# A macaron decoder layer on one core: paired matmuls in a new order, row sums at later pieces, and extra matmuls on a constant tile at the start

## The reference, cut to what matters

```python
def rmsnorm(x, gain):
    inv = lax.rsqrt(jnp.mean(xf * xf, axis=-1, keepdims=True) + EPS)
    return (xf * inv * gain)
def swiglu(h, w_gate, w_up, w_down):
    return (jax.nn.silu(h @ w_gate) * (h @ w_up)) @ w_down
...
x = x + 0.5 * swiglu(rmsnorm(x, norm_ffn1), w1_gate, w1_up, w1_down)
h = rmsnorm(x, norm_mix)
q, k, v, u = split(h @ w_in)             # 8 heads of 128, and 4 pooling groups of 256
attn = attention(rope(q), rope(k), v)    # causal over the 256 tokens
pooled = multiscale_pool(u, pool_w, pool_scale)
x = x + concatenate([attn, pooled]) @ w_out
x = x + 0.5 * swiglu(rmsnorm(x, norm_ffn2), w2_gate, w2_up, w2_down)
return rmsnorm(x, norm_final)
```

## Time and profile before

| | |
|---|---|
| median of 3 runs | 1843.48 us (1834.06, 1843.48, 1844.43) |
| profiled execution, its own time | 1844.73 us |
| span of that execution, first to last instruction | 1842.9 us |
| PE busy | 1807.6 us, 98% of the span |
| DVE, ACT, POOL busy | 1064.7, 853.8, 57.0 us |
| mean granted TensorE clock | 0.993 |

### The profile page before, as it was taken

How to read it: one execution, slowest core, us unless ns; L and a number is a source line. 1 busy time by engine, 2 the same in 40 slices (tenths; PEclk the granted TensorE clock), 3 DMA queues, 4 the chain that set the end, 5 groups by cost and what they waited for, 6 DMA issues and landing times.

```text
span 1842.9 us, 26110 instructions
## 1 busy us (share of the span) xinstructions
PE 1807.6 (98%) x10134; PEld 1566.5 (85%) x10134; DVE 1064.7 (58%) x1073; ACT 853.8 (46%) x993; POOL 57.0 (3%) x56
## 2 busy tenths in 40 slices
PE   6999999999999999999999999999999999999997
PEld 5888888888888888888787888888888888888886
DVE  5655555555555555577665656555555555545453
ACT  5444444444444444444544554444444444444443
POOL 2000000000000000000030010000000000000000
PEclk9999999999999999999999999999999999999999
DMA  7455555555555656756534555555555555565552
GB/s 253 161 185 188 190 188 182 182 183 184 185 160 183 190 178 188 241 185 193 170 124 128 187 187 179 187 191 186 182 182 184 187 189 172 170 183 183 187 187 91
DMA packets 214377, 333.41 MB, mean 181 GB/s; under 512 B 6104, under 2 KB 97472, under 8 KB 214336
## 3 DMA queue, kind: packets, MB, share of 16 engines
q1 hardware_dynamic: 212624, 331.37, 56.2%
q10 hardware_dynamic: 1712, 1.48, 0.3%
HBM read 330.73 MB, written 2.10 MB: 181 GB/s over the span
## 4 chain that ended last, share of the span: by engine, by line
PE 96%; DVE 1%; ACT 1%; issue 1%; DMA 1%; POOL 0%; SPq 0%
PE banks L330 61%; PE banks L332 31%; PE banks L424 1%; PE banks L422 1%; PE banks L423 1%; DMA raw<-in_w_gate 1%; PE banks L471 0%; PE banks L435 0%; ACT w_hi L564 0%; DVE w_lo L800 0%; POOL square_sum L1127 0%; PE banks L545 0%; PE banks L352 0%; PE banks L457 0%; ACT squares L590 0%
## 5 line engine op out<-in xcount | busy, mean ns | idle before, releaser
L800 DVE TENSOR_TENSOR w_lo<-raw,w_hi 128x1024 fp32r<-128x1024 f32 (+1 forms) x704 | 781.8, 1115 | 734.2 <-ACT w_hi L564 733.7
L330 PE MATMUL banks<-act,w_hi 128*128 128x512 f32 x3200 | 1135.3, 400 | 9.7 <-DVE u L854 2.9
L564 ACT ACTIVATE w_hi<-raw 128x1024 fp32r<-128x1024 f32 (+1 forms) x704 | 677.8, 963 | 947.3 <-PE banks L332 912.9
L332 PE MATMUL banks<-act,w_lo 128*128 128x256 f32 x3200 | 901.1, 282 | 0.0
L330 PEld LDWEIGHTS banks<-act,w_hi 128*128 128x128 f32 x3200 | 604.1, 189 | 159.2 <-DVE u L854 3.1
L332 PEld LDWEIGHTS banks<-act,w_lo 128*128 128x128 f32 x3200 | 608.1, 190 | 0.0
L330 PE MATMUL banks<-h,w_hi 128*128 128x512 f32 x1664 | 589.9, 400 | 3.5 <-DVE u L854 3.5
L332 PE MATMUL banks<-h,w_lo 128*128 128x256 f32 x1664 | 468.4, 282 | 0.0
L330 PEld LDWEIGHTS banks<-h,w_hi 128*128 128x128 f32 x1664 | 313.5, 188 | 81.9 <-DVE u L854 3.9
L332 PEld LDWEIGHTS banks<-h,w_lo 128*128 128x128 f32 x1664 | 315.6, 190 | 0.0
L854 DVE TENSOR_TENSOR h<-banks,h 128x1024 f32 (+1 forms) x44 | 53.7, 1220 | 0.7 <-ACT h L570 0.4
(11 more groups left out here) (111 smaller groups left out, 411.1 us busy)
## 6 DMA issues: line engine op xcount, KB each, us to landing
raw<-in_w_up SPq DMA_DIRECT2D x88, 1024.0 KB, 5.2
raw<-in_w_gate SPq DMA_DIRECT2D x87, 1024.0 KB, 5.2
raw<-in_w_down SPq DMA_DIRECT2D x64, 768.0 KB, 4.5
raw<-in_w_down SPq DMA_DIRECT2D x64, 640.0 KB, 4.2
raw<-in_w_in SPq DMA_DIRECT2D x32, 1024.0 KB, 5.4
raw<-in_w_out SPq DMA_DIRECT2D x16, 1024.0 KB, 5.0
rows<-in_x SPq DMA_DIRECT2D x4, 512.0 KB, 7.6
out<-rows SPq DMA_DIRECT2D x4, 512.0 KB, 3.1
```

The source lines that it names most:

```text
L330: pe.matmul(banks[:, bank + b, :], w_hi[:, s, w], operand[:, k, :], start=first, stop=last, skip_group_check=True)
L332: mm = pe.matmul(banks[:, bank + b, 0:S], w_lo[:, s, w], operand[:, k, 0:S], start=False, stop=last, skip_group_check=True)
L564: act_e.activation(w_hi[:, s, 0:n], raw[:, (p // 2) % RAW_SLOTS, off:off + n], ACT.Copy).then_inc(hi_ready, 1)
L800: dve.tensor_tensor(w_lo[:, s, 0:n], raw[:, (p // 2) % RAW_SLOTS, off:off + n], w_hi[:, s, 0:n].bitcast(F32), ALU.subtract)\
```

## The change

1. Inside a piece, PE issues for each output block first the long matmuls of all its channel blocks and then the short ones, in place of long, short, long, short.
2. In the first gate turn of both feed-forwards PE goes on with up pieces 8 to 11, then takes the sum (now in bank 0, once quad 0 has been read out), then pieces 12 to 15, and waits for the mean behind piece 15. DVE takes the mean behind piece 14 and the inverse behind piece 15; ACT takes the root behind piece 15 and the SiLU behind that. The middle's sum moves from behind Q0's last piece to behind K0's fourth, and the first rotation steps on DVE move with it.
3. DVE sets two tiles of `h` to 1.0 first of all. PE runs 7 matmuls on them (128 weight columns, 512 moving) ahead of the first transpose, and 4 more with 127 weight columns between the first 16 transposes and the first piece. Their products, in bank 3, are overwritten.

The core of the diff:

```diff
@@ multiply (PE), called for every piece
                 for b in range(width // P):
+                    cols = [slice(j * width + b * P, j * width + (b + 1) * P)
+                            for j in range(len(tiles))]
                     for j, k in enumerate(tiles):
-                        w = slice(j * width + b * P, j * width + (b + 1) * P)
-                        first, last = k == k_first, k == last_tile
-                        pe.matmul(banks[:, bank + b, :], w_hi[:, s, w], operand[:, k, :],
-                                  start=first, stop=last, skip_group_check=True)
-                        mm = pe.matmul(banks[:, bank + b, 0:S], w_lo[:, s, w],
-                                       operand[:, k, 0:S], start=False, stop=last,
+                        pe.matmul(banks[:, bank + b, :], w_hi[:, s, cols[j]], operand[:, k, :],
+                                  start=k == k_first, stop=k == last_tile, skip_group_check=True)
+                    for j, k in enumerate(tiles):
+                        mm = pe.matmul(banks[:, bank + b, 0:S], w_lo[:, s, cols[j]],
+                                       operand[:, k, 0:S], start=False, stop=k == last_tile,
                                        skip_group_check=True)
@@ gate_up (PE)
-                if first:
-
-                    if f["turn"]:
-                        pe.wait_ge(quad_read, m)
-                    sum_squares(0 if f["turn"] == 0 else 2, False)
...
-                        pe.wait_ge(gains_ready, 2)
-                    pe.wait_ge(meansq_ready, 1 if f["turn"] == 0 else 3)
+                if f["turn"] or not first:
+                    pe.wait_ge(quad_read, m)
                 else:
-                    pe.wait_ge(quad_read, m)
+                    pe.wait_ge(x_copied, 8)
                 for p in range(8, 16):
                     multiply_sb(turn, p, 1)
+                    if first and p == 11:
+                        pe.wait_ge(quad_read, m + 1)
+                        sum_squares(0 if f["turn"] == 0 else 2, False)
...
+                if first:
+
+                    pe.wait_ge(meansq_ready, 1 if f["turn"] == 0 else 3)
+                    if f["turn"] == 0:
+                        pe.wait_ge(gains_ready, 2)
@@ middle (PE)
-                        if p == K0:
+                        if p == Q1:
 
                             pe.wait_ge(meansq_ready, 2)
...
-                        if p == K0 - 1:
-                            pe.wait_ge(quad_read, MID_SB)
+                        if p == K0 + 3:
+                            pe.wait_ge(quad_read, MID_SB + 1)
                             sum_squares(1, True)
@@ the start (PE)
+            def warm(count, cols):
+
+                for _ in range(count):
+                    pe.matmul(banks[0:cols, 3, :], h[:, FT - 1, 0:cols], h[:, FT - 2, :],
+                              start=True, stop=True)
+
+            pe.wait_ge(warm_ready, 1)
+            warm(7, P)
             pe.wait_ge(first_const_landed, 16 * 2)
...
             turn_x(1)
+            warm(4, P - 1)
@@ gate_up (ACT)
-                    if first and p == 11:
-                        square_roots(0 if fresh else 2)
-                    if p == 14:
+                    if p == 14 and not first:
                         silu(SB * i)
+                if first:
+
+                    square_roots(0 if fresh else 2)
+                    act_e.wait_ge(gate_scaled, fi + 1)
+                    silu(SB * i)
@@ gate_up (DVE)
-                    if first and p == 10:
+                    if first and p == 14:
                         mean_square(norm)
...
-                    if p == 12:
+                    if p == (15 if first else 12):
                         if first:
                             inverse_root(norm)
@@ middle (DVE; ACT's square_roots(1) moves from p == 11 to p == 15)
-                    if p == 10:
+                    if p == 14:
                         mean_square(1)
...
-                    if 11 <= p < K1 + 16 and 3 <= p % 8 <= 7:
+                    if 19 <= p < K1 + 16 and 3 <= p % 8 <= 7:
                         rotate((p - 11) // 8, p % 8 - 3)
+                    if p in FIRST_ROTATE:
+                        rotate(0, FIRST_ROTATE.index(p))
@@ the start (DVE), and the tables
+            dve.memset(h[:, FT - 2:FT, :].bitcast(F32), 1.0).then_inc(warm_ready, 1)
+SUM_BANK = (0, 0, 0, 4)
+FIRST_ROTATE = (11, 15, 16, 17, 18)
```

More of the change, by code:

```diff
@@ L165, in layer_kernel @@
         ones_ready = sem("ones_ready")
+        warm_ready = sem("warm_ready")
         gains_turned = sem("gains_turned")
@@ L348, in sum_squares @@
                 pe.wait_ge(ones_ready, 1)
-                b = 4
+                b = SUM_BANK[norm]
                 if norm < 3:
@@ L383, in gate_up @@
                     multiply_sb(turn, p, 0, act_from=f["act"] if first else None)
-                if first:
-                    if f["turn"]:
-                        pe.wait_ge(quad_read, m)
-                    sum_squares(0 if f["turn"] == 0 else 2, False)
[L389 to L392, removed]
-                        pe.wait_ge(gains_ready, 2)
-                    pe.wait_ge(meansq_ready, 1 if f["turn"] == 0 else 3)
+                if f["turn"] or not first:
+                    pe.wait_ge(quad_read, m)
                 else:
-                    pe.wait_ge(quad_read, m)
+                    pe.wait_ge(x_copied, 8)
                 for p in range(8, 16):
                     multiply_sb(turn, p, 1)
+                    if first and p == 11:
+                        pe.wait_ge(quad_read, m + 1)
+                        sum_squares(0 if f["turn"] == 0 else 2, False)
+                        if f["turn"] == 0:
+                            pe.wait_ge(const_landed, 16 * 4)
+                            pe.transpose(banks[:, 1, 0:3 * KT + 8], gain_rows[:, :],
+                                         ident[0:3 * KT + 8, 0:3 * KT + 8]).then_inc(gains_turned, 1)
+                if first:
+                    pe.wait_ge(meansq_ready, 1 if f["turn"] == 0 else 3)
+                    if f["turn"] == 0:
+                        pe.wait_ge(gains_ready, 2)
             def down_two(f, i):
@@ L706, in middle @@
                         pair_update(ffns[0], KT - 2, DOWN_PAIRS - 1, MID_TURN * TURN, 1)
-                    if p == 11:
+                    if p == 15:
                         square_roots(1)
@@ L816, in mean_square @@
                 if norm in COL_NORMS:
-                    ins = dve.tensor_scalar(r_col[:, :], banks[:, 4, S:S + 2], 1.0 / D, EPS,
+                    ins = dve.tensor_scalar(r_col[:, :], banks[:, SUM_BANK[norm], S:S + 2], 1.0 / D, EPS,
                                             ALU.mult, ALU.add)
                 if norm in ROW_NORMS:
-                    ins = dve.tensor_scalar(r_row[:, :], banks[:, 4, 0:S], 1.0 / D, EPS,
+                    ins = dve.tensor_scalar(r_row[:, :], banks[:, SUM_BANK[norm], 0:S], 1.0 / D, EPS,
                                             ALU.mult, ALU.add)
@@ L870, in gate_up @@
                         feed(0, 2 * p, 2, 2 * p)
[L871 to L874, removed]
                     if first and f["turn"] and p in (3, 6):
@@ L880, in gate_up @@
                         split_h(SB * i - SB, fi)
-                    if first and p == 10:
+                    if first and p == 14:
                         mean_square(norm)
+                        if fresh:
+                            dve.wait_ge(gains_turned, 2)
+                            dve.tensor_copy(gains[:, KT:4 * KT + 8],
+                                            banks[:, 1, 0:3 * KT + 8]).then_inc(gains_ready, 1)
                     if p == 11:
                         add_half(0, h32[:, bass.ds(SB * i, SB), 0:S], m + 1, m + 1)
-                    if p == 12:
+                    if p == (15 if first else 12):
                         if first:
```

## The result

The changed kernel took 1814.65 us (median of 4 runs, 1812.41 to 1815.50; the profiled execution 1815.50, span 1813.7). The kernel before took 1838.77 us in the 4 runs beside it (1828.75 to 1844.43). The ratio of comparable runs is 0.992 with a 95% interval of 0.9892 to 0.9949: a gain of some 0.8%. Against the medians it is 1.3%, and against the one execution of before that was profiled 1.6%. That these three differ is the main finding of this study: the kernel before has three times, not one. (By that ratio before stands at some 1829 us, near the lowest of its four runs, 1828.75; a run list is therefore given wherever it matters.)

A forecast was written before the change was run, and what follows sets the result against it. PE, busy 98% of the span, bounds the kernel through how it issues and where it stands still. 1844.73 - 8.9 (first sum) + 0.5 (lateness) - 1.2 (other sums) - 29.9 (runs of two) = 1805 us; range 1798 to 1836.

The forecast's parts named there:

- The 0.70: Chance given to the changed kernel being faster, meaning a time below 1825 us.
- Two paces at one clock, drawn at a restart and kept: PE's long-short pairs run slow or fast, 7 ns a pair apart, set when PE restarts, held until the next interruption.
- The sum is made against the profiled execution, ... 1.25 us above the median: Baseline of the forecast: the profiled execution of the kernel before, 1844.73 us, 1.25 us above the median of three runs.
- Runs of two: Two long, then two short matmuls: all 4457 slow pairs in both feed-forwards go from 353.1 to 346.4 ns, -29.9 us.
- the V pieces' 226.7 ns: V pieces, all matmuls 512 columns: 213.3 ns plus 13.4 surcharge each; two surcharges on 320 ns give the fast pace, 346.7.
- The first sum, -8.9 us and +0.25: First gate turn: PE runs pieces 8 to 11 instead of waiting, -8.9 us; possible lateness afterwards booked as +0.25 us twice.
- The feared lateness of the SiLU: Root, inverse and SiLU behind piece 15 just hidden: next piece ready at 12.3 us, PE there at 12.5 or 12.2.
- The other two sums, -1.2: Middle and feed-forward 2: PE's waits of 0.63 and 0.52 us behind the sums go, -1.2 us.
- The start, 0: Memset and constant-tile matmuls ahead of the first piece cost nothing, taken as 0 between -1 and +1.7 us.
- the order doesn't matter: Rival: surcharge belongs to PE's restart state, pairs stay at 353 ns, only waits go, 1835 us; chance 0.13.
- short behind short is dearer: Rival: 2624 short matmuls behind short ones cost extra, from 3.7 ns each slower, 1861 us at 10 ns; chance 0.10.
- the pace is mixed: Rival: half the excess stays in both feed-forwards, or one falls in a slow pace, 1819 to 1821 us; chance 0.25.

The follow-up runs named there:

- experiment 10: The kernel before, unchanged, in one single execution for another trace: 1832.79 us.
- 6: The changed kernel without all 11 matmuls on the constant tile: 1813.51 us (4 runs, 1812.43 to 1815.51).
- 7: The changed kernel with 128 weight columns in place of 127 in the four matmuls ahead of the first piece: 1813.56 us (4 runs).
- experiment 1: The kernel before with runs of two and nothing else: 1825.52 us (12 runs, 1824.29 to 1826.90).
- 5: The kernel before with sums moved, long and short alternating, gains turned ahead of the first turn's sum: 1807.11 us (7 runs, one of them 1819.82).
- 9: Sums moved, alternating, gains turned ahead of the sum, run again for a second trace: 1806.72 us (6 runs, one of them 1819.85).
- 2: The changed kernel with long and short alternating and without the 11 constant-tile matmuls (sums moved alone): 1821.05 us (12 runs, 1819.16 to 1822.66).
- experiment 3: The changed kernel with long and short alternating, constant-tile matmuls kept: 1822.67 us (8 runs 1820.04 to 1822.80, 4 runs 1831.09 to 1832.64).

## Why the prediction was wrong

It said 1805 us, 2.1% below the median then known; the changed kernel took 1814.65. That lies inside the range from 1798 to 1836, but the gain is 0.8% (1.0% against the median of the 75 times of before), less than half of the forecast's. The 0.70 stood for a time below 1825 us, which came; that bound was 1% below 1843.48 us, though, and the same time is no more than 1.0% below 1832.9. Two steps failed, of nearly the same size: of the 38.5 us from 1843.5 to 1805, 10.6 were never there (1843.5 less 1832.9) and 9.6 stayed (1814.65 less 1805).

*Two paces at one clock, drawn at a restart and kept*: right, and now shown in traces of the same code with 0, 1 and 2 fast feed-forwards.

*"The sum is made against the profiled execution, ... 1.25 us above the median"*: this is the first step that failed. The profiled execution had drawn slow twice, as by their times 29 of 75 runs do. It even had the other pace within it: behind the middle's sum, from 797.4 to 863.9 us, 192 pairs took 347.1 ns each. The text saw that a restart draws the pace and that the three runs spanned 10 us, used the span only to weigh a rival, and then let all 4457 pairs of one draw count as the kernel's. At the usual draw, one feed-forward slow, about half of the 29.9 us was never there to gain. A kernel with two paces has to be forecast against the mixture: 1832.9 us, from which the forecast's own result of 1805 would have been 1.5%.

*Runs of two, "if the new order always runs at the surcharge of 13.4 ns", -29.9 us*: the second step that failed, in its size. The new order does always run at one pace, but in place of 346.4 ns at 348.3 in the gate and up pieces and at 349.4 in the down projections ((754.88 - 508.92) / 704 from the starts of its first pair and of Q0's), 348.8 over the 2111 pairs behind the first sum. 4457 pairs x 2.4 ns are 10.7 us, about what the time missed by. Between the second gate turn and Q0 it brought 9.0 us (-17.7 less -8.7), from feed-forward 2's second turn on 9.2, and some 2 in the middle and in the turn before: 20 us against the slow draws. The fast pace of alternating matmuls (346.7 by the starts) is better than it; runs of two buy evenness, not speed. What made me take 346.4 was the V pieces' 226.7 ns, which carried over neither to runs of two (233) nor of eight (230). In the V pieces the activations are the stationary operand and the weights move (`banks<-w_hi,act`), so they are another kind of matmul; whether that is the reason is not shown. That two V surcharges gave the fast pace was luck: in the fast stretches of experiment 10 a long matmul takes 230.0 ns and a short one 116.7, which is 16.7 and 10.0 above their columns and not 13.4 twice. What was read right is where the slow pace's excess stands: in the slow stretches of before a long one takes 236.6 and a short one again 116.7.

*The first sum, -8.9 us and +0.25*: measured -8.7 at the second gate turn, where the pace had still had no time to tell. The feared lateness of the SiLU had 1.7 us in hand, because the table is loaded ahead of the wait.

*The other two sums, -1.2*: about -0.7 in the middle (Q0 to Q1 is 1.0 us shorter, 0.3 of it pace) and -0.8 in feed-forward 2 (1.4 us over its first turn, 0.6 of it pace). Right.

*The start, 0*: right; experiments 6 and 7 are 1.1 us below the changed kernel, within its spread of 3 us.

*Not in the forecast*: between V0's end and W0 the changed kernel lost 2.7 us. PE waits 2.9 and 3.5 us for DVE there in both kernels; the granted clock was 0.50 for 3.4 us (from 898.4) and for 6.8 us (from 929.1) in the changed kernel, and for 3.4 us (from 948.3) in the kernel before, which had another 3.4 us behind W0 (from 979.0). So 2.8 us came back between W0 and feed-forward 2. It doesn't seem to be of the change: the run with four matmuls of 128 columns, the same code otherwise, had one such stretch of 3.4 us in the middle (from 957.8) and came to W0 4.3 us earlier, to feed-forward 2 2.7 us.

*The rivals*: "the order doesn't matter" fell (experiment 1), "short behind short is dearer" too (0.115 us, 119 ns in eights), "the pace is mixed" was right for before, the one place where it wasn't applied. The Trainium skill, in "TensorE: Matmul & The Clock Gate", section "LDWEIGHTS (loading the stationary operand)", gives a load as columns / 1.2, an estimate of 107 ns for 128. The traces do not speak against it: short matmuls, each with a load of its own, start 115 to 119 ns apart.

## What to carry to other kernels

Before forecasting from one trace, look whether the same code runs at two paces within it; if so, the profiled execution is one draw, and the baseline is the list of runs with its clusters. Then separate an edit that removes time in every draw (the moved sums: 10 us between the two traces, 12 between experiments 1 and 6) from one that changes the draws (runs of two: 12 runs within 3 us of each other, but with the sums moved 8 us slower than the usual draw of experiments 5 and 9). The best kernel found here keeps long and short alternating, with sums moved and the gains turned ahead of the sum: 1807.1 and 1806.7 us, 7.5 and 7.9 us below the changed kernel, at the price of one run in six or seven at 1820.

## What was unexpected about the hardware

Alternating matmuls of 512 and 256 columns, each with its own weights, ran for 700 us on end at either 353.3 or 346.7 ns a pair, at the same granted clock (1.00), in the same code and with the same transfers; in these traces it changed at interruptions of PE alone. A 56-row transpose ahead of or behind the sum's two matmuls (four rows in the trace) moved the odds, told by the times, from 0 of 12 to 11 of 13 runs. Which property of the restart decides was not found: the same last rows led to both paces (experiments 5 and 9). One rival is left untested there: that with the gains first the pace just goes on over the sum, and was drawn at piece 8. In the four traces with moved sums pieces 8 to 11 ran at 353.3 (2), 346.5 (3), 353.3 (5) and 346.7 ns (9), and the rest of feed-forward 1 at 353.3, 353.3, 353.3 and 346.7: both traces with the gains first kept their pace, and with the sum first experiment 3 went from fast to slow. It is no rule for every sum: in feed-forward 2 of 2, 3 and 9 a slow stretch went over into a fast one. Why runs of two have a single pace, and why it lies 2 ns a pair above the fast one, is open as well.
